# Joint down quarters of a hybrid decoder step: a weight ring that holds two pairs' blocks

## What is computed

```python
def rms_norm(x, g):
    xf = x.astype(jnp.float32)
    y = xf * lax.rsqrt(jnp.mean(xf * xf, axis=-1, keepdims=True) + RMS_EPS)
    return (y * g.astype(jnp.float32)).astype(x.dtype)
...
    x = x + rms_norm(mixed, g_mix_post)
    h = rms_norm(x, g_mlp_pre)
    u = jnp.square(jax.nn.relu(jnp.einsum('btd,df->btf', h, w_up)))
    x = x + rms_norm(jnp.einsum('btf,fd->btd', u, w_down), g_mlp_post)
    return x, s_new, k_a, v_a
```

## Time and profile before

| | |
|---|---|
| median of 3 runs | 1635.44 us (1629.28 to 1636.02) |
| the profiled execution | 1635.0 us, its span 1633.2 us |
| TensorE matmuls, busy | 1532.6 us (94%) |
| VectorE, busy | 1119.8 us (69%) |
| ScalarE, busy | 822.9 us (50%) |
| GpSimd, busy | 213.6 us (13%) |
| mean granted TensorE clock | 0.976 of full |

### The profile page before, as it was taken

One profiled execution on the slowest core, in us unless ns is written; L12 is line 12 of the kernel. 1 busy time (PEld: TensorE's weight loads), 2 busy tenths in 40 slices (PEclk: granted clock), 3 DMA queues, 4 the chain that ended last, 5 costly groups with the idle time before them and its releaser, 6 DMA issues.

```text
span 1633.2 us, 30105 instructions
## 1 busy us (share of the span) xinstructions
PE 1532.6 (94%) x11792; PEld 1454.5 (89%) x11792; DVE 1119.8 (69%) x2032; ACT 822.9 (50%) x1581; POOL 213.6 (13%) x224
## 2 busy tenths in 40 slices
PE   7999999999999799699999999999999996987996
PEld 6898789988999789699999987898899996987996
DVE  6774777755587667578778557877556776666765
ACT  7446554564554324346664565556645452342553
POOL 2220133000001121210003100510010012113000
PEclk9999999999999899799999999999999998998998
DMA  6545744442542121135544566345335402311562
GB/s 210 195 149 172 273 154 134 164 149 93 166 143 65 51 93 65 53 120 186 181 147 130 168 226 220 118 130 194 109 120 165 131 25 78 121 36 52 173 222 78
DMA packets 76328, 222.74 MB, mean 136 GB/s; under 512 B 7923, under 2 KB 25715, under 8 KB 76060
## 3 DMA queue, kind: packets, MB, share of 16 engines
q1 hardware_dynamic: 76188, 220.81, 40.6%
HBM read 208.97 MB, written 14.44 MB: 137 GB/s over the span
## 4 chain that ended last, share of the span: by engine, by line
PE 79%; DVE 9%; ACT 4%; DMA 4%; issue 3%; SPq 0%; DVEq 0%; ACTq 0%
PE ps L1270 53%; PE ps L1324 8%; PE ps L1267 6%; DMA w_raw<-w 3%; PE ps L1363 2%; DVE w_rest L1632 2%; PE ps L1513 1%; PE ps L1500 1%; PE ps L1528 1%; ACT w_high L892 1%; DVE w_rest L1639 1%; DVE reg L1763 1%; ACT w_high L901 1%; DVE norm_every L1748 1%; DMA kc<-kcT 1%
## 5 line engine op out<-in xcount | busy, mean ns | idle before, releaser
L1270 PE MATMUL ps<-h_high,w_rest 128*128 128x320 f32 (+1 forms) x1888 | 569.6, 302 | 3.8 <-DVE w_rest L1632 2.4
L1270 PE MATMUL ps<-h_rest,w_high 128*128 128x320 f32 (+1 forms) x1888 | 559.3, 296 | 0.0
L1270 PE MATMUL ps<-h_high,w_high 128*128 128x320 f32 (+1 forms) x1888 | 559.2, 296 | 0.0
L1632 DVE TENSOR_TENSOR w_rest<-w_raw,w_high 128x1024 fp32r<-128x1024 f32 x300 | 372.0, 1248 | 40.4 <-ACT w_high L892 40.0
L1270 PEld LDWEIGHTS ps<-h_high,w_rest 128*128 128x128 f32 x1888 | 359.0, 190 | 19.4 <-issue 11.2
L892 ACT ACTIVATE w_high<-w_raw 128x1024 fp32r<-128x1024 f32 x304 | 317.1, 1051 | 114.1 <-PE ps L1270 76.4
L1270 PEld LDWEIGHTS ps<-h_rest,w_high 128*128 128x128 f32 x1888 | 359.1, 190 | 0.5
L1270 PEld LDWEIGHTS ps<-h_high,w_high 128*128 128x128 f32 x1888 | 359.0, 190 | 0.0
L1270 PE MATMUL ps<-u_high,w_rest 128*128 128x320 f32 (+1 forms) x512 | 153.5, 300 | 0.0
L1270 PE MATMUL ps<-u_high,w_high 128*128 128x320 f32 (+1 forms) x512 | 151.7, 296 | 0.0
L1270 PE MATMUL ps<-u_rest,w_high 128*128 128x320 f32 (+1 forms) x512 | 151.7, 296 | 0.0
(11 more groups left out here) (247 smaller groups left out, 2669.5 us busy)
## 6 DMA issues: line engine op xcount, KB each, us to landing
w_raw<-w SPq DMA_DIRECT2D x336, 512.0 KB, 3.6
kc<-kcT SPq DMA_DIRECT2D x16, 512.0 KB, 8.2
vc<-vc SPq DMA_DIRECT2D x16, 512.0 KB, 7.6
s_in<-s SPq DMA_DIRECT2D x8, 512.0 KB, 6.4
ss<-s_in SPq DMA_DIRECT2D x8, 512.0 KB, 5.9
bias<-rel_scratch SPq DMA_DIRECT2D x8, 512.0 KB, 6.0
rel_scratch<-rel_row SPq DMA_DIRECT2D x1, 2560.0 KB, 14.1
bias<-rel_scratch SPq DMA_DIRECT2D x8, 256.0 KB, 5.2
```

The source lines that it names most:

```text
L1270: last = pe.matmul(ps[:, bank, 0:n], wt[:, slot, c, :], xt[:, c, :], **flags)
L1632: V.tensor_tensor(wlo[:, v % RING], raw[:, v % RING], whi[:, v % RING].bitcast(F32), ALU.subtract).then_inc(S["w_lo_d"], 1)
```

## The change

1. **Ring.** Pairs' blocks now go to `raw[v % RING]`: pairs 0 and 2 to slots 0 and 1, pairs 1 and 3 to slots 2 and 3. They count on the ordinary semaphores `w_in0` to `w_in3`. The sums S1, S2 and S4 of pair 0 stay in slots 2 and 3; those of pairs 1 to 3 go to a new tile `w_sums`, which lies over `u_a`. S3 is made in place.
2. **Waits of the loads.** Pair 1's blocks wait for six low parts of pair 0 (through S4), pair 2's for all seven of pair 0, pair 3's for all of pair 1. The next up quarter's first two blocks wait for pair 2 and the other two for pair 3.
3. **Waits of the sums.** Those of pair 1 wait for its blocks and for all mixed u of the quarter (`t_raw`), those of pairs 2 and 3 for six low parts of the pair before.
4. **Order.** Weight parts 6 and 7 are made after the last parts of u, on ScalarE and on VectorE.
5. **Place.** The sums of pair 0 are issued at the first unit of the up quarter instead of the seventh.

```diff
-ENTRY_AT = ((0, 0), (1, HC), (0, HC), (2, 0), (2, HC), (3, 0), (1, 0))
+BLOCK_AT = {E_A11: (0, 0), E_A22: (1, HC), E_A12: (0, HC), E_S3: (1, 0)}
+SUM_AT = {E_S1: (2, 0), E_S2: (2, HC), E_S4: (3, 0)}
...
+    s_tile = place("w_sums", [P, 3, HC, P], offset=o_states)
...
-    def entry_source(i):
-        slot, c = ENTRY_AT[i]
+    def entry_source(p, i):
+        if i in SUM_AT and p % HC:
+            return s_tile[:, sorted(SUM_AT).index(i)]
+        slot, c = SUM_AT[i] if i in SUM_AT else BLOCK_AT[i]
+        slot += 0 if i in SUM_AT else 2 * (p % 2)
         return raw[:, slot, c:c + HC, :]
...
             def raw_free(v):
 
-                if v in pair_of:
-                    if pair_of[v] % HC == 0:
-                        sp.wait_ge(S[lo_of[v - RING][0]], lo_of[v - RING][1])
-                    else:
-                        sp.wait_ge(S["j_lo"], PRODUCTS * pair_of[v])
-                elif v - RING in pair_of:
-                    sp.wait_ge(S["j_lo"], PRODUCTS * HC * (pair_of[v - RING] // HC + 1))
+                if v - RING in pair_of:
+                    sp.wait_ge(S["j_lo"], PRODUCTS * (pair_of[v - RING] + 1))
                 else:
                     sp.wait_ge(S[lo_of[v - RING][0]], lo_of[v - RING][1])
+                    if v in pair_of and pair_of[v] % HC:
+                        sp.wait_ge(S["j_lo"], PRODUCTS * (pair_of[v] - 1) + E_S4 + 1)
...
                         if p % HC == 0:
-                            v = min(v for v in pair_of if pair_of[v] == p)
                             for u in (v - 2, v - 1):
                                 pool.wait_ge(S[lo_of[u][0]], lo_of[u][1])
+                        elif p % HC == 1:
+                            pool.wait_ge(S["t_raw"], 4 * HC * (p // HC + 1))
                         else:
-                            pool.wait_ge(S["j_lo"], PRODUCTS * p)
+                            pool.wait_ge(S["j_lo"], PRODUCTS * (p - 1) + E_S4 + 1)
...
-                elif mixed_u(o) and o.h and o.k == KC - 2:
+                elif mixed_u(o) and o.h and o.k == 0:
                     sums(HC * quarter(o), range(4))
...
                 if o.k == 0:
                     mix_high(o.l, o.tile, HC - 1, range(4))
+                    for e in (ENTRIES - 2, ENTRIES - 1):
+                        half_high(p + e // PRODUCTS, e % PRODUCTS)
...
+                        if v + RING in pair_of and v % RING == RING - 1:
+                            continue
...
                 if o.k == 0:
                     mix_rest(o.l, o.tile, HC - 1, range(4))
+                    for v in late:
+                        rest_or_halves(v)
...
                 if o.kind == "J":
-                    for v in late:
-                        rest_or_halves(v)
-                    pair(o, before)
+                    pair(o, before, late)
```

More of the change, by code:

```diff
@@ L547, in build @@
     hi_no = {v: n + 1 for n, v in enumerate(single)}
-    in_no = {v: sum(u % RING == v % RING for u in single[:n + 1]) for n, v in enumerate(single)}
+    block_of = {o.evn: o.loads[0] for o in outs if o.kind == "J"}
     lo_of = {v: ("w_lo_p", v) if v else ("w_lo_0", 1) for v in range(RING)}
@@ L614, in load @@
             def load(v):
[L615 to L618, removed]
+                sp.dma_start(raw[:, v % RING].rearrange("p a b -> p (a b)"),
+                             w[loads[v]:loads[v] + 1].rearrange("o p n -> p (o n)")).then_inc(S[f"w_in{v % RING}"], 16)
             def raw_free(v):
-                if v in pair_of:
-                    if pair_of[v] % HC == 0:
-                        sp.wait_ge(S[lo_of[v - RING][0]], lo_of[v - RING][1])
-                    else:
-                        sp.wait_ge(S["j_lo"], PRODUCTS * pair_of[v])
-                elif v - RING in pair_of:
-                    sp.wait_ge(S["j_lo"], PRODUCTS * HC * (pair_of[v - RING] // HC + 1))
+                if v - RING in pair_of:
+                    sp.wait_ge(S["j_lo"], PRODUCTS * (pair_of[v - RING] + 1))
                 else:
                     sp.wait_ge(S[lo_of[v - RING][0]], lo_of[v - RING][1])
+                    if v in pair_of and pair_of[v] % HC:
+                        sp.wait_ge(S["j_lo"], PRODUCTS * (pair_of[v] - 1) + E_S4 + 1)
             load(0)
@@ L853, in sums @@
                 for n in which:
-                    s1, s2, s4, s3 = (entry_source(e) for e in (E_S1, E_S2, E_S4, E_S3))
-                    a11, a12, a22 = (entry_source(e) for e in (E_A11, E_A12, E_A22))
+                    s1, s2, s4, s3 = (entry_source(p, e) for e in (E_S1, E_S2, E_S4, E_S3))
+                    a11, a12, a22 = (entry_source(p, e) for e in (E_A11, E_A12, E_A22))
                     if n == 0:
-                        pool.wait_ge(S["j_in0"], 16 * (p + 1))
-                        pool.wait_ge(S["j_in1"], 16 * (p + 1))
+                        v = block_of[p]
+                        for u in (v, v + 1):
+                            pool.wait_ge(S[f"w_in{u % RING}"], 16 * (u // RING + 1))
                         if p % HC == 0:
-                            v = min(v for v in pair_of if pair_of[v] == p)
                             for u in (v - 2, v - 1):
                                 pool.wait_ge(S[lo_of[u][0]], lo_of[u][1])
+                        elif p % HC == 1:
+                            pool.wait_ge(S["t_raw"], 4 * HC * (p // HC + 1))
                         else:
-                            pool.wait_ge(S["j_lo"], PRODUCTS * p)
+                            pool.wait_ge(S["j_lo"], PRODUCTS * (p - 1) + E_S4 + 1)
                         V.tensor_tensor(s1, s3, a22, ALU.add).then_inc(S["j_sum"], 1)
@@ L890, in high @@
             def high(v):
-                act.wait_ge(S[f"w_in{v % RING}"], 16 * in_no[v])
+                act.wait_ge(S[f"w_in{v % RING}"], 16 * (v // RING + 1))
                 A.activation(whi[:, v % RING], raw[:, v % RING], ACT.Copy).then_inc(S["w_hi"], 1)
@@ L896, in half_high @@
                 if i in (E_A11, E_A12, E_A22):
-                    act.wait_ge(S["j_in1" if i == E_A22 else "j_in0"], 16 * (p + 1))
+                    v = block_of[p] + (1 if i == E_A22 else 0)
+                    act.wait_ge(S[f"w_in{v % RING}"], 16 * (v // RING + 1))
                 else:
@@ L900, in half_high @@
                 e = (PRODUCTS * (p % HC) + i) % ENTRIES
[L901 removed]
+                A.activation(half_block(whi, e), entry_source(p, i), ACT.Copy).then_inc(S["j_hi"], 1)
             def mix_high(l, q, c, which):
@@ L1671, in pair_squares, with pair @@
                     add_square(norm_no(o.l, 3, 0), k, WIDE[0])
-            def pair(o, before):
+            def pair(o, before, late):
                 p, first = o.evn, PRODUCTS * HC * (o.evn // HC)
```

5 lines of the change are left out of this document (2 added, 3 removed).

## The result

The changed kernel takes 1588.07 us (median of 4 runs, 1584.01 to 1589.36), the kernel before 1634.99 beside it (4 runs, 1629.28 to 1636.02): a ratio of 0.9716, 95% interval 0.9687 to 0.9745. The forecast was 1589. The profiled span went from 1633.2 to 1585.5 us, 47.7 less.

A forecast was written before the change was run, and what follows sets the result against it. TensorE works 94% of the span, so only its idle or half-clock time in the joint down quarters could be saved: 19.1 + 29.6 - 2.4 = 46.3 us, 1635.4 to 1589, range 1577 to 1607.

The forecast's parts named there:

- Pairs 1 and 2: Second and third pairs of the four joint down quarters: the wider ring removes their waits, 29.6 us.
- late evictions: Pairs' product 0 evictions come only 0.3 to 0.4 us early; priced 0.3 us per pair, 8 pairs, 2.4 us lost.
- Rival (a): VectorE and GpSimd become the bound in pairs 1 and 2, costing 10 to 18 us: 1599 to 1607; chance 0.17.
- The entry: Start of each quarter, pair 0: product 2 starts 4.8 us earlier, 19.1 us in four quarters (16.4 to 22.0).
- the tie: Quarter's entry: fourth low part of u at 546.89 against GpSimd at 546.9; middle of held and unheld taken, product 2 at 552.3.
- The order (part 2): Quarter's entry: u's last sums go ahead of weight parts; product 1's wait for the mix falls from 5.66 to 0.4 us.
- The clock: Product 2 to the end of pair 0: the 8.9 us paid at half clock stay, no gain (bounds 0, and 6 more).
- Rival (b): The clock doesn't fall at the entry, giving back 8.9 us: 1580, with the unheld entry 1571; chance 0.10.
- Rival (c): Pair 1's blocks still arrive late at the entry; at most 8 of the 19.1 us are left: 1600; chance 0.08.
- Rival (d): The half clock level stays on through the quarters, slower than before: over 1700; chance 0.03.
- The rule against this change: Entry: exclusive lock between GpSimd and VectorE operations with two SBUF inputs; without it the time would be 9 us less.
- Outside the quarters: Rest of the kernel: nothing should move by more than a microsecond or two.

The follow-up runs named there:

- place_back: Changed kernel with pair 0's sums issued at the seventh unit of the up quarter again: 1584.57 us, one run.
- order_only: Kernel before plus only the new order (weight parts 6 and 7 after the last parts of u): 1622.65 us, ratio 0.9946 to the kernel before.
- ring_only: Changed kernel with the new order undone, weight parts 6 and 7 ahead of u's last sums again: 1589.23 us, ratio 0.9747 to the kernel before.
- sums_late: Changed kernel, pair 1's GpSimd sums also waiting for pair 1's first low part (the eighth weight part): 1571.67 us, ratio 0.9640 to the kernel before.
- load_late: Changed kernel with pair 1's load waiting for all seven low parts of pair 0 again: 1595.18 us, one run.
- evict_mid: Changed kernel with sums_late's wait and product 0 evicted ahead of weight parts 6 and 7: 1573.09 us, ratio 0.9644 to the kernel before.
- evict_tlo: Changed kernel, product 0 evicted ahead of weight parts 6 and 7, pair 1's sums waiting for u's four low parts: 1574.33 us, ratio 0.9632 to before.
- evict_only: Changed kernel with product 0 evicted behind u's four low parts and ahead of the two weight parts: 1574.78 us, one run.

## Why the prediction was right, and where its steps were off

The total (46.3 us forecast, 47.7 in the span, of which 44.4 in the quarters) is right within 2 us. The mechanism is the one forecast, but that the number is so close is partly luck: the pairs gave 2.0 us more than their terms and the entry 3.1 less, the clock took 0.8, and 3.3 came from outside.

- **Pairs 1 and 2: 29.6 us forecast, and 2.4 off for late evictions; 29.25 measured.** The term is right; the price of 2.4 was too high. The slack that I had worked out is there: in the first quarter's pair 2, product 0's evictions end at 574.60 and product 1 at 574.97. Having worked out 0.3 to 0.4 us of slack, I nevertheless charged 0.3 us per pair; 0.37 us were lost in all eight. Rival (a) fell with it: VectorE is busy 19.86 of 22.77 us and TensorE all of it.
- **The entry: 19.1 us forecast (16.4 to 22.0), 16.0 measured.** The load and the first sum came where the steps had them (sum 3.97 us into the quarter, forecast 4.04), the wait for the mix is 0.4 us as forecast. The step that failed is the tie: the fourth low part of u came at 4.15 and not at 4.03, so it was held in all four quarters and not in half of them, and the two weight parts took 1.75 and 1.74 us, not 1.4. The lower end of the range, everything held (product 2 at 10.14), is what came: 10.18 to 10.26. That it agrees to 0.1 us is luck in part: the first weight part ended at 7.35 us, 0.14 earlier than in that sum, and the second at 9.02, 0.13 later. place_back shows the other side once, at 9.11. Where a tie is decided by 0.05 us in a sum of estimates, the end with the loss was the one to take: a middle that no quarter can show has no mechanism behind it.
- **The order (part 2).** The steps credited it with bringing the mix early, and summed both parts together. Alone on the kernel before it is worth 11.9 us of the quarters (order_only), on top of the ring nothing (ring_only). The prediction nowhere asked what each part gives without the other; the sum did not need it, but a reader would have taken from it that both were needed. Its own rows had the answer: six VectorE operations lie ahead of the eviction in either order.
- **The clock: 0 forecast, 0.8 us lost**, within the bounds. Rival (b) did not come true: the idle piece was 5.85 us and the clock fell at it in all four quarters. With 2.7 us in sums_late half of it came true, two quarters out of four. The prediction's sign for (b), a piece of 2.46 us that left the clock at full level, was one side of its own trace. In pairs 1 and 2 of the kernel before, eight idle pieces of 2.10 to 2.86 us stand ahead of a product 2, and behind four of them the clock fell; one, of 2.10 us, is in the same first quarter:

```profile
588.20:591.61 3.41, 3.41 (x16) 3.41 (x15) 2.39 (x4) 0.63 (x1) 3.33 (x3) 0.50 0.00 0
```

By these rows the price of (b) with an unheld entry, all of the 8.9 us, was too high: about half of it, by four of eight, is my estimate now. sums_late gave 5.8.

- **Rival (c)** (blocks late at the entry) fell by the load at 538.66. load_late made it on purpose: it costs 3.8 us of the quarters by its profile, and not the 11 that I had priced it at (19.1 less 8).
- **Rival (d)** (half level lasting) did not occur: full clock from pair 1 on in all quarters.
- **The rule against this change.** The forecast gave 9 us as what an entry without holding would save at the clock of before. sums_late shows 12.7 at product 2 (since more was held than forecast), and 5.8 more behind it, by the clock.
- **Outside the quarters** nothing was forecast to move by more than a microsecond or two; 3.3 us did, ahead of the first quarter: 6.8 us at half clock that the profile of before has there and that of the changed kernel has not. Left out, the kernel would stand at about 1591, still within 2 us of the forecast.

The chances put 0.62 on a time from 1580 to 1598, and it came there by the mechanism named.

## What to carry to other kernels

Widening a buffer makes its producers start early, and they can then run at the very moment when another engine has short, urgent work on the same memory. In this kernel they did. After adding the buffer, ask what now runs beside the critical entry, and hold it back by a wait on the work that it would disturb: one wait line gave another 0.8% here. Two edits that both shorten the wait ahead of one operation need not add up (here 11.5 and 16.3 us at product 2 alone, 16.0 together); count how much work of the next engine stays in front of it, in either order.

## What the runs showed of the hardware

- VectorE's fp32 operations with both inputs in SBUF and GpSimd's sums take turns. A 128x256 low part of 0.42 us took 1.52 beside a sum, a 128x512 one of 0.69 us took 1.4 to 1.8, and about one such operation is held for each sum. GpSimd is held as well: its 128x512 sum takes 1.27 us alone, 1.3 to 1.6 with low parts of 128x256 between and 1.6 to 1.75 with those of 128x512. The Trainium skill (SBUF — State Buffer, section "SBUF: two separate sides") states an exclusive lock for such pairs, which whoever starts first keeps for the whole instruction. The trace agrees: the low part of u at 543.66, beside the sum of 543.48 to 544.90, ended at 545.19. Evictions from PSUM with one SBUF input (0.47 us at 548.45, with a sum under way from 547.94 to 549.65) were not held by it.
- I had not expected that four idle pieces of the same 2.7 us, at the same place of the same loop, would be followed by granted clocks of 0.82, 1.00, 0.82 and 1.00 (sums_late). Behind 5.85 to 5.92 us the clock was 0.73 to 0.76 in all four quarters of the changed kernel; behind 1.4 us it was 1.00 in all four of evict_mid and of evict_tlo; behind 2.52 us in evict_only it was 1.00 once and 0.82 twice. A piece of 2.13 to 2.14 us ahead of the first quarter stands in all ten profiles, near 302, and behind it the clock fell in three (before, load_late, evict_only). What decides at 2.1 to 2.9 us stays open.
- Where the clock fell at a wait of TensorE, the half level cost 1.2 us (sums_late, 9.44 against 8.22) to 2.5 us (the changed kernel, 10.37 against 7.86) beside the idle time, and nothing where VectorE was the limit (evict_only, 9.60 against 9.62).
